# Cached values loaded from another queue, score groups one tile earlier, and gathers paced by turns

## The reference, cut to what matters

```python
c_past = cache_kv_latent[l][page_table].reshape(DB, past, KV_LORA)   # 8 pages of 128 rows x 256
kr_past = cache_k_rope[l][page_table].reshape(DB, past, QK_ROPE)     # the same pages, 64 wide
...
def mem_attend(h, mk, mv, w_xq, w_xo):
    q = (h @ w_xq).reshape(B, T, MEM_HEADS, MEM_HEAD_DIM)
    s = jnp.einsum('bthd,bmhd->bhtm', q, mk).astype(jnp.float32) * MEM_SCALE
    p = jax.nn.softmax(s, -1).astype(mv.dtype)
    o = jnp.einsum('bhtm,bmhd->bthd', p, mv).reshape(B, T, MEM_HEADS * MEM_HEAD_DIM)
    return o @ w_xo
...
xp = xp + mem_attend(rmsnorm(xp, norm_x[l]), mk, mv, w_xq[l], w_xo[l])          # keys, values computed
xs = xs + mem_attend(rmsnorm(xs, norm_x[l]), cache_mem_k[l], cache_mem_v[l], w_xq[l], w_xo[l])  # cached
```

## Time and profile before

| | before |
|---|---|
| median of 3 runs | 880.54 us |
| profiled execution, its own time | 878.88 us |
| its span | 877.1 us |
| PE busy | 800.4 us (91%) |
| DVE busy | 494.0 us (56%) |
| ACT busy | 331.9 us (38%) |
| POOL busy | 115.7 us (13%) |
| DMA | 109.94 MB, mean 125 GB/s |

### The profile page before, as it was taken

How to read it: one execution, slowest core, us unless ns; L and a number is a source line. 1 busy time by engine, 2 the same in 40 slices (tenths; PEclk the granted TensorE clock), 3 DMA queues, 4 the chain that set the end, 5 groups by cost and what they waited for, 6 DMA issues and landing times.

```text
span 877.1 us, 16001 instructions
## 1 busy us (share of the span) xinstructions
PE 800.4 (91%) x6463; PEld 764.3 (87%) x6463; DVE 494.0 (56%) x1073; ACT 331.9 (38%) x730; POOL 115.7 (13%) x161
## 2 busy tenths in 40 slices
PE   5989998778979996699899899999999999999994
PEld 4979987655869996698799899999999999999994
DVE  5578465668575477665356565556665554322322
ACT  5313676612263323455333333333333332222312
POOL 0366103030172111000044000000000000000000
PEclk9999997999989999799999999999999999999997
DMA  7412336060575667954423143332333332332312
GB/s 217 131 50 79 91 99 264 1 263 26 169 264 187 217 176 232 319 168 129 138 80 90 56 116 94 97 92 82 92 97 97 96 98 85 115 90 85 90 43 98
DMA packets 141408, 109.94 MB, mean 125 GB/s; under 512 B 8983, under 2 KB 133872, under 8 KB 138255
## 3 DMA queue, kind: packets, MB, share of 16 engines
q1 hardware_dynamic: 134471, 90.32, 33.7%
q0 software_dynamic: 3104, 14.68, 5.2%
q10 hardware_dynamic: 3760, 3.92, 1.3%
HBM read 103.93 MB, written 5.20 MB: 124 GB/s over the span
## 4 chain that ended last, share of the span: by engine, by line
PE 62%; DMA 4%; DVE 2%; ACT 1%; issue 1%; ACTq 0%; SPq 0%; DVEq 0%
PE ps L2051 19%; PE ps L2052 19%; PE ps L2053 19%; DMA wraw<-in_w_mk_dram 2%; DMA wraw<-in_w_mv_dram 1%; PE ps L2555 1%; PE ps L2510 1%; PE ps L2512 1%; PE ps L2511 1%; DMA kv_slot<-in_cache_mem_v_dram 1%; PE ps L2630 0%; PE ps L2458 0%; DVE wlo L1465 0%; DVE rstd L1488 0%; DVE prod L1845 0%
## 5 line engine op out<-in xcount | busy, mean ns | idle before, releaser
L2051 PE MATMUL ps<-B_hi,whi 128*128 128x260 f32 x992 | 282.2, 284 | 9.3 <-DVE wlo L1465 3.7
L2052 PE MATMUL ps<-B_lo,whi 128*128 128x260 f32 x992 | 280.7, 283 | 0.0
L2053 PE MATMUL ps<-B_hi,wlo 128*128 128x260 f32 x992 | 280.2, 283 | 0.0
L1465 DVE TENSOR_TENSOR wlo<-wraw,whi 128x512 fp32r<-128x512 f32 (+1 forms) x262 | 178.6, 724 | 168.4 <-ACT whi L964 165.6
L964 ACT ACTIVATE whi<-wraw 128x512 fp32r<-128x512 f32 (+1 forms) x262 | 147.5, 613 | 209.5 <-PE ps L2053 157.7
L2051 PEld LDWEIGHTS ps<-B_hi,whi 128*128 128x128 f32 x992 | 187.5, 189 | 10.6 <-issue 7.9
L2052 PEld LDWEIGHTS ps<-B_lo,whi 128*128 128x128 f32 x992 | 187.7, 189 | 0.1
L2053 PEld LDWEIGHTS ps<-B_hi,wlo 128*128 128x128 f32 x992 | 187.6, 189 | 0.0
L2052 PE MATMUL ps<-h_lo,whi 128*128 128x260 f32 x352 | 99.7, 283 | 0.0
L2051 PE MATMUL ps<-h_hi,whi 128*128 128x260 f32 x352 | 99.4, 282 | 0.0
L2053 PE MATMUL ps<-h_hi,wlo 128*128 128x260 f32 x352 | 99.4, 282 | 0.0
(11 more groups left out here) (413 smaller groups left out, 1230.4 us busy)
## 6 DMA issues: line engine op xcount, KB each, us to landing
wraw<-in_w_gate_dram SPq DMA_DIRECT2D x22, 512.0 KB, 3.9
wraw<-in_w_up_dram SPq DMA_DIRECT2D x22, 512.0 KB, 3.8
kv_slot<-in_cache_mem_k_dram SPq DMA_DIRECT2D x8, 1024.0 KB, 8.6
kv_slot<-in_cache_mem_v_dram SPq DMA_DIRECT2D x8, 1024.0 KB, 6.9
wraw<-in_w_down_dram SPq DMA_DIRECT2D x16, 512.0 KB, 3.6
wraw<-in_w_out_dram SPq DMA_DIRECT2D x14, 512.0 KB, 4.0
wraw<-in_w_in_dram SPq DMA_DIRECT2D x9, 512.0 KB, 4.0
wraw<-in_w_xq_dram SPq DMA_DIRECT2D x8, 512.0 KB, 6.3
```

The costliest lines, as they stand in the source:

```text
L1465: return dve.tensor_tensor(dst, src, high.bitcast(F32), ALU.subtract)
L2051: pe.matmul(dst, left[0], right[0], start=first, stop=False)
L2052: pe.matmul(dst, left[0], right[1], start=False, stop=False)
L2053: return pe.matmul(dst, left[1], right[0], start=False, stop=last)
```

## The change

Three edits. The groups of cached scores are put together anew and each starts one tile sooner (`m >= 3`, and `5 + j` at the key tiles; group 8 now stands before `cmaxes(0)`). The eight value loads leave SP's program and stand in POOL's, behind its last broadcast: values 0 and 4 after group 7's second half, 1 and 2 after the first half of group 8, 3 and 5 after its second half, 6 and 7 as before after `v_used` 5 and 6. Each cached load has a semaphore of its own. The gathers of samples 5, 6 and 7 wait for "turned 1", "turned 2" and "turned 3".

```diff
-           [[(2, 0), (2, 1)], [(2, 2)]], [[(2, 3), (2, 4)], [(3, 3), (3, 4)]],
-           [[(2, 5), (2, 6)], [(3, 5), (3, 6)]], [[(3, 0), (3, 1)], [(3, 2)]],
-           [[(0, 7), (1, 7)], [(2, 7), (3, 7)]]]
+           [[(2, 0), (2, 1)], [(2, 2)]], [[(2, 3), (2, 4)], [(2, 5), (2, 6)]],
+           [[(0, 7), (1, 7)], [(2, 7)]], [[(3, 0), (3, 1)], [(3, 2), (3, 3)]],
+           [[(3, 4), (3, 5)], [(3, 6), (3, 7)]]]
...
+        def load_cached(eng, n):
+            src = a["cache_mem_k" if n < NB else "cache_mem_v"][0, n % NB]
+            dst = kv_slot[(K_SLOT + V_SLOT)[n]]
+            eng.dma_start(dst[:, :, :], src.rearrange("(p m) h d -> p m (h d)", m=2)).then_inc((k_in + v_in)[n], 16)
...
             for i in range(2, len(MEM_TILES) + 2):
                 load_w(S_MEM + i)
-                if i in (4, 6, 8, 9):
-                    spent(sp, {4: 5, 6: 6, 8: 7, 9: 8}[i], 1)
-                for b in {4: (0,), 5: (1,), 6: (2,), 7: (3,), 9: (4,), 10: (5,)}.get(i, ()):
-                    load_kv(NB + b)
-                if i == 16:
-                    sp.wait_ge(v_used, 5)
-                    load_kv(NB + 6)
-                if i == 17:
-                    sp.wait_ge(v_used, 6)
-                    load_kv(NB + 7)
...
-                elif b == 7:
-                    gp.wait_ge(val, VAL["turned", 1] + 1)
+                elif b >= 5:
+                    gp.wait_ge(val, VAL["turned", b - 4] + 1)
...
+            for g, half, values_of in ((7, 1, (0, 4)), (8, 0, (1, 2)), (8, 1, (3, 5))):
+                spent(gp, g, half)
+                for b in values_of:
+                    load_cached(gp, NB + b)
+            for b in (6, 7):
+                gp.wait_ge(v_used, b - 1)
+                load_cached(gp, NB + b)
             squares("nf", "xo2", range(KD), lambda c: xT[:, c, :])
...
-                if m >= 4:
-                    scores_of(m - 4)
+                if m >= 3:
+                    scores_of(m - 3)
...
                 key_tile(j)
-                scores_of(4 + j)
+                scores_of(5 + j)
             cmaxes(0)
-            scores_of(8)
```

More of the change, by code:

```diff
@@ L550, in build @@
         past_mixed = sem("past_mixed")
-        kv_in = [sem(f"kv_in{i}") for i in range(8)]
+        k_in = [sem(f"k_in{b}") for b in range(NB)]
+        v_in = [sem(f"v_in{b}") for b in range(NB)]
         mv_half = sem("mv_half")
@@ L721, in by_row @@
             return bank[:, 0:2 * P].rearrange("p (d h x) -> p d h x", d=2, h=NH)[:, :, :, 0:NB]
[L723 to L726, removed]
         def spent(eng, g, i):
@@ L732, in cached @@
         def cached(eng, n):
-            i = (K_SLOT + V_SLOT)[n]
-            eng.wait_ge(kv_in[i], kv_count[n])
-            return kv_slot[i]
+            eng.wait_ge((k_in + v_in)[n], 16)
+            return kv_slot[(K_SLOT + V_SLOT)[n]]
+        def load_cached(eng, n):
+            src = a["cache_mem_k" if n < NB else "cache_mem_v"][0, n % NB]
+            dst = kv_slot[(K_SLOT + V_SLOT)[n]]
+            eng.dma_start(dst[:, :, :], src.rearrange("(p m) h d -> p m (h d)", m=2)).then_inc((k_in + v_in)[n], 16)
         def rows_of(t):
@@ L788, in _ @@
             sp.wait_ge(lo, SPLIT["uvs",] + 1)
[L789 to L792, removed]
             for s in range(S_OUT + 3, S_XQ + 2):
@@ L799, in _ @@
                 elif s < S_OUT + 8:
-                    load_kv(s - S_OUT - 5)
+                    load_cached(sp, s - S_OUT - 5)
             full(sp, ("o", KD - 1, 1))
             for b in range(3, 7):
-                load_kv(b)
+                load_cached(sp, b)
                 load_w(S_XQ + b - 1)
@@ L807, in _ @@
             full(sp, ("xq", KD - 1, 1))
-            load_kv(7)
+            load_cached(sp, 7)
             for i in range(2, len(MEM_TILES) + 2):
                 load_w(S_MEM + i)
-                if i in (4, 6, 8, 9):
-                    spent(sp, {4: 5, 6: 6, 8: 7, 9: 8}[i], 1)
-                for b in {4: (0,), 5: (1,), 6: (2,), 7: (3,), 9: (4,), 10: (5,)}.get(i, ()):
-                    load_kv(NB + b)
-                if i == 16:
-                    sp.wait_ge(v_used, 5)
-                    load_kv(NB + 6)
-                if i == 17:
-                    sp.wait_ge(v_used, 6)
-                    load_kv(NB + 7)
             for s in range(S_XO + 2, NSLOT):
```

## The result

The changed kernel is slower: 888.61 us in the median of five runs (886.53 to 890.56) against 882.51 (878.08 to 883.03) for the kernel before, a ratio of 1.0091 with a 95% interval of 1.0056 to 1.0126. A second series, beside the experiments, gave 1.0143 (1.0105 to 1.0181). The forecast was 880.2, with a range up to 886.

The account below looks back on a forecast made before the run. PE bounds the kernel nearly everywhere; from 329 to 373 us three slow weight transfers make it wait. From the profiled 878.88 us, +2.9 ("cdiag" later) and -1.6 (gathers) gave 880.2; likeliest range 877 to 884, overall 870 to 886.

Parts of the forecast that it names:

- DVE's new order: Score groups from 330.5: values 0 and 4 may start at 345.4, tile 7 issued 346.7, "cmx" at 352.5 instead of 357.9.
- Tile 7's landing: Weight load before "cdiag": beside the value burst lands at 364.5, so "cdiag"'s matmul starts at 369.4, 2.9 us later.
- Value 7: 0: PE's 0.7 us wait for value 7: from POOL's queue it may land up to 0.5 us later or earlier, priced 0.
- The same again: PE's clock after idling before "cdiag": same loss as before, some 1.3 us, already in the sum; at worst +1.7.
- A lag of "about 1 us at most" for tile 2: Two broadcasts issued before SP's load of key 7, 0.5 MB ahead of it, shift everything by about 1 us at most.
- Gathers: Pacing the gathers of samples 5 to 7 may remove DVE's 4.96 us stall before 191.49: -1.6 us, bounds 0 and -3.3.
- The third rival: Tile 7 starved until the value burst's end (+4.1), PE cold longer (+1.7), gathers 0: 884.7 to 885.2 us; chance 0.12.

## Why the prediction was wrong

- **DVE's new order** was right. Values 0 and 4 may start at 341.4 and tile 7 is issued at 342.72; the last query projection ended 4.5 us sooner than before (317.0), and relative to it both are within 0.5 us of the forecast 345.4 and 346.7. The 5.3 us for "mv 0" fell to 0.4 as said.
- **Tile 7's landing**: the mechanism was right and its size was not. Turns by packets stretch it, as the earlier trace rows had shown, and the matmul behind "cdiag" comes later although "cmx" comes sooner. I had +2.9 us and it was +4.8: the end of the last query projection to that matmul is 49.8 us against 45.0. I took 314 rows in 5 us, 63 in a microsecond, from a stretch where queue 0's packets held 6.0 KB on average (1.86 MB in 310). The values' held 7.6 (1.55 MB in 205, 350 to 354 us), and the rows got 51 turns in a microsecond, and 48 with ACT's store, which I had not counted, in the round. The larger packets are most of the difference, the store the rest. By 360 us, when the burst was nearly through, 771 of the 1024 rows had moved, and the others took until 361.9.
- **"Value 7: 0"** was the step that failed. I said, without a row, that another queue moves a landing by half a microsecond at most. From issue to landing it took 7.3 us against 5.4, and 8.8 in the second profile; the wait grew from 0.69 to 2.85 and 4.3 us. With value 7 back on SP's queue it took 5.8 us and the wait 1.05. Why it is slower on POOL's is not shown.
- **"The same again" for the clock** failed with it. I priced only the place before "cdiag", where the loss was about 1 us more. Behind value 7 I had no wait and so no loss; there the run with values 6 and 7 on SP puts it at 2 to 3 us. In the profiled execution the longer wait (2.2 us) and the clock behind it (2.9) are 5.1 of the 6.3 us that lie between the forecast's +1.3 and the measured +7.6.
- **A lag of "about 1 us at most" for tile 2** failed. Four query broadcasts now stand ahead of key 7 and two beside tile 2, where there were two and one. Its load took 8.3 us in one profile and 10.9 to 12.6 in six others with the same groups and key 7 ahead, against 6.55. The first profile of the changed kernel has the smallest of these, which may be why it lies below the median of 888.61. I took the broadcasts' bytes for their price, against what the turns on tile 7 had warned of. Which broadcasts do it, and how, is not settled: the one profile with two of them held has 8.87 us, inside the 8.3 to 12.6 of those without.
- **Gathers**: -1.6 forecast, -3.7 measured, past my bound of -3.3. I had halved the gain since the trace named no releaser; the two runs with the one edit show that the stall goes with them.

The sum for the profiled execution: 1.0 us of ordinary difference before the gathers, then 3.7 gained; 0.8 lost before the last query projection, 7.4 up to value 7, 2.9 behind it and 1.3 in the rest. The third rival had this outcome nearly (884.7 to 885.2), with the starved tile and the cold clock in it, but it put the cold clock in the wrong place and gave the gathers nothing, so part of its nearness is luck. Its landing of tile 7 did come: counted from the end of the last query projection, 361.93 is 366.4 on the forecast's clock, and it was to decide from about 366 on. The tile got there by slower turns, though, and not behind the whole burst. I gave the rival 0.12, because the earlier trace rows spoke against a whole burst ahead of the tile. The rest of the slower side came from value 7, the clock behind it and tile 2, terms that I had each set to about nothing.

## What to carry to other kernels

A load on a queue of its own does not yield to urgent loads: where its packets stood waiting here, it took every second or third turn, and a turn cost what its packets cost. Where small rows are on the critical path, keep the large loads behind them in the same queue; that was worth 1.2 to 1.9% here, with the times of the loads changed along with the queue. The Trainium skill, "DMA: Bandwidth & Descriptors", section "Issuing engines are not separate DMA queues", says that spreading issues over engines saves only their issue time; in these runs the move gained nothing that shows in the time, and it cost. When you price a transfer beside others, count the packets of every queue then active, and count a wait of PE with the clock behind it.

## What was not expected of the hardware

- Three queues share by packets too: 289, 288 and 240 in 6 us, for 8 KB, 512 B and 1 KB each, and 185, 182 and 186 in 4 us for 8 KB, 1 KB and 1 KB. Tile 7, 1024 rows of 512 B, landed in 3.6 us alone, in 19.0 to 19.2 beside values in packets of 8 KB, and in 22.95 with old groups, where broadcasts go just ahead of the values. Pieces of 1 KB on POOL's queue went in packets of 4 KB, and beside the first of them tile 7 landed in 6.5 us without equal turns.
- With gathers that ran ahead DVE stood for 4.9 us with a releaser the profile calls "remote"; with the last three issued by turns the stall was gone. What in DVE waited for what is still not shown; only that it goes with the gathers is.
- A wait of PE of 2.5 us or more before a sparse stretch of 30 matmuls went with another 1.6 to 2.9 us behind it (in the changed kernel's two profiles at a granted clock of 0.65 and 0.73); one of 1.05 us went with none, at 1.00.
